# A two-block transformer kernel: the order of ScalarE's and VectorE's pieces in the second block's projections, one pair of gate-row loads on another queue, and two weight blobs exchanged

## What is computed

```python
proj = u @ w_in[l]
qa, ka, va, qb, kb, vb, g = jnp.split(proj, SPLITS, axis=-1)
qa = rope(qa.reshape(B, Lp, SWA_Q_HEADS, HEAD_DIM), pos)      # 16 heads of 64
ka = rope(ka.reshape(B, Lp, SWA_KV_HEADS, HEAD_DIM), pos)     # 4 heads
qb = rope(qb.reshape(B, Lp, DIFF_HEADS, 2, HEAD_DIM), pos)    # 8 heads, two parts each
kb = rope(kb.reshape(B, Lp, DIFF_HEADS, 2, HEAD_DIM), pos)
...
o_swa = windowed_gqa_sink_attention(qa, ka, va, attn_sink[l], pos, is_real)
lam = (jnp.exp(jnp.sum(lambda_q1 * lambda_k1)) - jnp.exp(jnp.sum(lambda_q2 * lambda_k2)) + lambda_init)
o_diff = differential_attention(qb, kb, vb, lam, lambda_init, diff_subln_gain[l], is_key)
gates = jax.nn.sigmoid(g + b_gate[l])
g_swa, g_diff = gates[..., :D_MODEL], gates[..., D_MODEL:]
merged = g_swa * (o_swa @ w_branch_swa[l]) + g_diff * (o_diff @ w_branch_diff[l])
h = h + rms_norm(merged @ w_out[l], post_mix_gain[l])
```

## Time and profile before

| | |
|---|---|
| median of three runs | 875.66 us (875.16 to 877.67) |
| the profiled execution, its own time | 876.87 us |
| its span, first to last instruction | 875.1 us |
| TensorE busy in it | 862.2 us, 99% |
| VectorE, ScalarE, GpSimd busy | 629.0, 468.0, 73.7 us |
| mean granted TensorE clock | 0.999 of full speed |
| HBM traffic | 184 GB/s over the span |

### The profile page before, as it was taken

One profiled execution on the slowest core, in us unless ns is written; L12 is line 12 of the kernel. 1 busy time (PEld: TensorE's weight loads), 2 busy tenths in 40 slices (PEclk: granted clock), 3 DMA queues, 4 the chain that ended last, 5 costly groups with the idle time before them and its releaser, 6 DMA issues.

```text
span 875.1 us, 13099 instructions
## 1 busy us (share of the span) xinstructions
PE 862.2 (99%) x4820; PEld 737.9 (84%) x4820; DVE 629.0 (72%) x985; ACT 468.0 (53%) x756; POOL 73.7 (8%) x96
## 2 busy tenths in 40 slices
PE   8999999999999999999999999999999999999997
PEld 6887788888888888889889888788888888888886
DVE  5867677766876666668778887888766876666665
ACT  6546534434644444444566887676653654444443
POOL 1000000000200000002322010133300100000000
PEclk9999999999999999999999999999999999999999
DMA  9955344554565555352798443755474365455531
GB/s 331 400 212 192 116 169 149 192 188 149 186 241 191 192 192 192 144 192 86 259 274 288 136 157 117 246 192 172 169 269 173 122 225 190 177 198 188 189 143 48
DMA packets 31774, 167.21 MB, mean 191 GB/s; under 512 B 4128, under 2 KB 5920, under 8 KB 14320
## 3 DMA queue, kind: packets, MB, share of 16 engines
q1 hardware_dynamic: 28992, 159.17, 51.8%
q10 hardware_dynamic: 2736, 7.42, 2.4%
HBM read 157.02 MB, written 3.83 MB: 184 GB/s over the span
## 4 chain that ended last, share of the span: by engine, by line
PE 86%; DVE 6%; ACT 3%; DMA 1%; issue 1%; POOL 1%; SPq 0%; ACTq 0%; DVEq 0%
PE ps L522 16%; PE ps L524 16%; PE ps L523 16%; PE ps L688 8%; PE ps L673 8%; PE ps L692 4%; PE ps L669 4%; PE ps L701 2%; DVE wlo L1859 2%; ACT whi L862 1%; PE ps L557 1%; PE ps L1755 1%; DMA kswap<-kraw 1%; PE ps L703 1%; PE ps L1713 1%
## 5 line engine op out<-in xcount | busy, mean ns | idle before, releaser
L1859 DVE TENSOR_TENSOR wlo<-raw,whi 128x2048 fp32r<-128x2048 f32 x134 | 307.4, 2295 | 146.3 <-ACT whi L862 145.9
L862 ACT ACTIVATE whi<-raw 128x2048 fp32r<-128x2048 f32 x134 | 256.2, 1913 | 180.0 <-PE ps L524 109.0
L522 PE MATMUL ps<-whi,xT 128*128 128x512 f32 x192 | 76.8, 400 | 0.0
L524 PE MATMUL ps<-whi,xT 128*128 128x512 f32 x192 | 75.0, 391 | 0.0
L523 PE MATMUL ps<-wlo,xT 128*128 128x512 f32 x192 | 74.8, 390 | 0.0
L1326 POOL TENSOR_TENSOR stat<-stat,cst 128x1 f32<-128x1 f32 x10 | 11.9, 1200 | 490.0 <-DVE stat L1879 261.0
L522 PE MATMUL ps<-whi,fT_h 128*128 128x512 f32 x128 | 50.2, 392 | 0.0
L523 PE MATMUL ps<-wlo,fT_h 128*128 128x512 f32 x128 | 49.8, 389 | 0.0
L524 PE MATMUL ps<-whi,fT_l 128*128 128x512 f32 x128 | 49.8, 389 | 0.0
L522 PE MATMUL ps<-x_all,whi 128*128 128x272 f32 x160 | 46.5, 291 | 1.6 <-DVE wlo L1859 1.5
L523 PE MATMUL ps<-x_all,whi 128*128 128x272 f32 x160 | 46.1, 288 | 0.0
(11 more groups left out here) (349 smaller groups left out, 1886.9 us busy)
## 6 DMA issues: line engine op xcount, KB each, us to landing
raw<-weights SPq DMA_DIRECT2D x134, 1024.0 KB, 4.8
kB<-key_parts SPq DMA_DIRECT2D x20, 272.0 KB, 3.5
kswap<-kraw SPq DMA_DIRECT2D x26, 136.0 KB, 2.5
key_parts<-knat SPq DMA_DIRECT2D x4, 544.0 KB, 7.3
cst<-consts SPq DMA_DIRECT2D x1, 1371.0 KB, 13.3
raw<-weights SPq DMA_DIRECT2D x4, 256.0 KB, 5.1
raw<-weights SPq DMA_DIRECT2D x2, 512.0 KB, 6.7
gate_a<-gain_rows ACTq DMA_DIRECT2D x2, 512.0 KB, 7.9
```

The costliest lines, as they stand in the source:

```text
L522: pe.matmul(o, lh, rh, start=first, stop=False)
L524: return pe.matmul(o, ll, rh, start=False, stop=last)
L862: act.activation(whi[s][:], raw[s][:], ACT.Copy).then_inc(split_hi, 1)
L1859: dve.tensor_tensor(wlo[s][:], raw[s][:], whi[s][:], ALU.subtract).then_inc(split_lo, 1)
```

## The change

1. ScalarE: `keys_high` at q = 4, 6, 8, 10, 12 goes from ahead of the unit's pieces to behind the high part of the same q.
2. ScalarE: `queries_high` goes from ahead of the unit's pieces to behind them, at the same odd q.
3. The gate rows 2 are issued by SyncE, behind the key loads of blob step 22, in place of ScalarE at q = 38. The wait for 16 units' scores is there already, in `load_keys(1)`.
4. Blob 11 becomes a query blob and blob 12 a values blob; `VALUES_AT` moves the turn of these values from q = 24 to 26, and `TAKERS` follows.
5. VectorE: `step_lambda` goes from q = 14 to q = 13, where it stands ahead of the low part of blob 8.

What is computed stays the same, and so do the number and the shapes of all operations.

```diff
--- before.py
+++ after.py
@@ -108,13 +108,13 @@
     return 2 * KC * r + 2 * XT_ORDER[r].index((t, k // 2 * 2)) + k % 2 + 1
 
 
-QUERIES = (6, 7, 9, 10, 12, 13, 15, 17)
+QUERIES = (6, 7, 9, 10, 11, 13, 15, 17)
 QUERY_PLACE = (0, 1, 4, 2, 3, 5, 6, 7)
-VALUES = (5, 8, 11, 14, 16)
+VALUES = (5, 8, 12, 14, 16)
 SWAPPED = (0, 1, 2, 3, 4) + QUERIES
 
 
-VALUES_AT = {12: 0, 18: 1, 24: 2, 30: 3, 34: 4}
+VALUES_AT = {12: 0, 18: 1, 26: 2, 30: 3, 34: 4}
 
 
 def pair_bank(m2):
@@ -484,7 +484,7 @@
 
 
         TAKERS = "aadd" + "aa" + "dd" + "dddd" + "dd" + "dd" + (
-            "aaaaa" + "a" + "dd" + "a" + "dd" + "a" + "dd" + "a" + "d" + "a" + "d" + "dd" + "dd" + "dd" + "dd")
+            "aaaaa" + "a" + "dd" + "a" + "ddd" + "a" + "d" + "a" + "d" + "a" + "d" + "dd" + "dd" + "dd" + "dd")
 
         def wait_pair_free(pe, group):
 
@@ -838,6 +838,9 @@
                     load_keys(0)
                 if 22 <= m < 29:
                     load_keys(m - 21)
+                if m == 22:
+                    for t in range(NT):
+                        sp.dma_start(gate_s[:, t, :], grow[5].partition_broadcast(P)).then_inc(bias_in[2], 16)
                 if m - 7 in QUERIES:
                     store_queries(m - 7)
                 if m - 4 in SWAPPED:
@@ -1150,10 +1153,6 @@
                     values_in(VALUES_AT[q - 1])
                 if q in VALUES_AT:
                     values_out(VALUES_AT[q])
-                if q in (4, 6, 8, 10, 12):
-                    keys_high(q // 2 - 2)
-                if q % 2 == 1 and (q - 5) // 2 in QUERIES:
-                    queries_high((q - 5) // 2)
                 if q == 14:
                     act.wait_ge(lam_s, 1)
                     act.activation(lam[:, 2:4], lam[:, 0:2], ACT.Exp).then_inc(lam_e, 1)
@@ -1204,9 +1203,8 @@
                     act.activation(dT_h[:, cc, t * P:(t + 1) * P], ps[:, 5, 3 * P:4 * P],
                                    ACT.Copy, scale=subgain[:]).then_inc(d_hi, 1)
 
-                if q == 38:
-                    act.wait_ge(u_sc, S_UNITS)
-                    bias_rows(2, gate_s)
+                if q % 2 == 1 and (q - 5) // 2 in QUERIES:
+                    queries_high((q - 5) // 2)
                 if q == 54:
                     act.wait_ge(u_sc, UNITS)
                     bias_rows(3, gate_d)
@@ -1220,6 +1218,8 @@
                     act.dma_start(gain_rows[:], grow[1:3].partition_broadcast(P)).then_inc(rows_in, 16)
                 if q % 2 == 0 and m:
                     hi(N1 + m + 2)
+                if q in (4, 6, 8, 10, 12):
+                    keys_high(q // 2 - 2)
                 if q == 2:
                     for t in range(NT):
                         act.wait_ge(h_ok, 9 + 2 * t)
@@ -2351,7 +2351,7 @@
 
             for q in range(2 * OUT2):
                 m2 = q // 2
-                if q == 14:
+                if q == 13:
                     step_lambda()
                 if q == 4:
                     take_rows(rrow2, 2, 5)
```

## The result

The changed kernel takes 880.26 us (median of 9 runs), the kernel before, run beside it, 875.66: a ratio of 1.0045, with a 95% interval from 1.0036 to 1.0054. By that ratio it is slower by about 4 us (the two medians lie 4.6 apart), and it lies above the predicted range of 872.6 to 878.9. The profiled execution takes 881.04 us, with a span of 879.3 in place of 875.1.

A forecast was written before the change was run, and what follows sets the result against it. TensorE was taken to bound the kernel, busy 862.2 of 875.1 us, with 4.6 us of waits to win. Terms +2.5 - 0.6 - 0.8 = +1.1 us gave a median of 876.8 us, range 872.6 to 878.9.

The forecast's parts named there:

- Weights parts ahead of key parts, q = 4 to 12: ScalarE's reordering: 0 at q = 4, TensorE's 1.5 us wait staying; about 1.5 us won at 443.6 (q = 12).
- my two signs of being wrong: Wrong if the wait at 488 isn't there, or if the swap of blob 6 lands before 453.
- What becomes of these 1.5 us: At blob 8's values, 457 to 458 us: TensorE, early, waits for a transfer, so only 0.3 of 1.5 us are left.
- the lambda step: VectorE, q = 14 to 13: swap of blob 6 issued 0.9 us later, priced at 0 as transfers land in issue order.
- Queries behind the exponentials, blobs 11 and 12 exchanged: q = 23 to 26: a longer chain makes TensorE reach unit 2 at 489.1, not 486.58; a loss of 2.5 us.
- What comes back: TensorE's waits at q = 30 and q = 40 go, winning 0.6 and 0.8 us.
- rival 3: `step_lambda` passes its wait on: swap of blob 6 lands 0.9 later, q = 40 keeps 0.8; +2.8, 878.5 us; chance 0.15.
- Rival 1: q = 20 to 24: query behind the exponentials is out of the way in time; -1.7, 874.0 us; chance 0.26.
- rival 2: Early gains kept: GpSimd isn't held at 417, everything runs 1.1 us ahead; -3.4, 872.3 us; chance 0.14.

The follow-up runs named there:

- keys_alone: Kernel before with only the key parts put behind the weights parts (q = 4 to 12): 878.81 us, ratio 1.0025.
- keys_last_only: Kernel before with only the last key part (q = 12) put behind the high part of blob 8: 875.14 us, ratio 0.9982.
- exchange_alone: Kernel before with only query blob 12 and values blob 11 exchanged: 878.06 us, ratio 1.0012.
- lambda_alone: Kernel before with only the lambda step at q = 13 in place of 14: 876.44 us, ratio 1.0000.
- low5_swap3_first: Kernel before plus changes 1 to 3, blob 3's swap ahead of weights, blob 5's low part ahead of the turn of keys 2: 877.51 us, ratio 1.0007.
- after_swap_first: Changed kernel with stores of keys 1 and 2 and swaps of blobs 3 and 4 ahead of weights of blobs 7 and 8: 876.46 us, ratio 1.0003.
- after_swap3_first: Changed kernel with only the store of keys 1 and the swap of blob 3 ahead of the weights of blob 7: 876.01 us, ratio 0.9994.
- after_queries_back: Changed kernel with the query parts back ahead of the exponentials, blobs 11 and 12 still exchanged: 879.80 us, ratio 1.0035.

## Why the prediction was wrong

**The step that failed** is "Weights parts ahead of key parts, q = 4 to 12". Up to blob 5 it was right almost to the figure: GpSimd's part took 2.65 (2.64 forecast), the turn of keys 2 started at 423.51 + 1.5 = 425.0 (425.1), the low part of blob 5 at 427.1 (427.2). Behind that I followed nothing until q = 12 and entered a gain of 1.5, of which 0.3 was to last. But GpSimd's part of keys 1 ended earlier (422.64 + 1.5 = 424.1, in place of 425.7), while the weights of blob 7 were issued 1.3 later, so its store and the swap of blob 3 went out right behind 1 MB of weights. The term was -1.5 for one wait; measured, that wait of 1.7 gave way to two with 3.7 in all, and the step alone costs 2.2 us (keys_alone). Taken back from the whole change it makes 3.3. Neither of my two signs of being wrong came up, as both look past this step: the wait at q = 26 is there, and the swap of blob 6 lands at 452.7 + 1.5 = 454.2.

**"What becomes of these 1.5 us"** failed too. With the wait gone, the gain stays (keys_last_only: -1.6), since the swap of blob 6 lands 3.2 us after its issue and doesn't hold TensorE at 458. I had taken landings of one execution for fixed times: behind the same transfers at the same distances the swap took 3.0 in exchange_alone. Nor did all transfers of that execution land in the order of issue, on which the 0 for the lambda step rested: the first half of this swap, issued at 446.61, landed after 3.1 us, at 449.7, ahead of the weights (451.1) and the keys (452.5).

**Queries behind the exponentials, blobs 11 and 12 exchanged:** the place was right and the size nearly so (a wait on the copy of values at q = 26, 1.8 for 2.3 forecast; 0.2 for 0.8 at 481). The cause was one of the two edits that the term priced together: the exchange puts the values at the end of a chain through the low part of blob 14 and unit 2's scaling, and makes the wait by itself (1.9 in exchange_alone), wherever query 10's copies stand. Without the exchange the queries' move, with the gate rows on SyncE, gains 1.1.

**What comes back** was right: no wait at q = 30 and 40. **The lambda step** at 0 agrees with lambda_alone; its interval doesn't rule out the 0.9 of rival 3, but the wait that this rival needs isn't there. Rival 1 fell with the wait at q = 26, and rival 2 with GpSimd's part, which was held (2.65 us); early gains came only with another order on SyncE.

**TensorE's clock** was no term at all. In the profile of after it accounts for most of what the waits don't: 5.7 us behind the start-up, against 3.0 more of waits. Sum of the forecast +1.1; measured about +4: 3.3 from the key parts and 0.6 from the rest, both with the clock in them. So the forecast was near for the rest, and what it lacked is the key parts. The parts don't simply add: timed alone they give +2.2, +1.1, -1.1 and 0, in sum 2.2.

## What to carry to other kernels

When an engine's work ends sooner, the transfers that hang on it are issued sooner too: look up what the queue holds ahead of them at that moment, since here a small transfer that others waited for came late behind a megabyte that nobody needed yet. Read how long a transfer takes from more than one profile before a step rests on it. Follow every link of a chain that is moved, not only the one at which a wait stood. When two edits of a change pull in different directions, time them apart: here the parts that gain, with the swaps put ahead of the weights, are worth 3.9 us without the others.

## What the runs showed of the hardware

The fall of the granted clock differs between executions of one kernel. In the 126 runs of the kernel before that were made beside the experiments, the mean granted clock was 0.998 or higher in 86 (median 876.0 us) and lower in 40 (877.7). Across kernels the share tends to go with the longest wait of the profile: lower in 0 of 12 for keys_last_only, whose longest wait is 1.5, in 7 of 9 for the changed kernel (2.4), in 10 of 11 for low5_swap3_first (4.6). But the waits don't settle it: after_swap_first and after_swap3_first have the same two of 1.9 in their profiles and are lower in 9 of 12 and 3 of 11. The three waits of 1.9 to 2.3 in the profile of after_queries_back had no fall behind them (granted clock 1.00 from 425 to 500). So a wait of about 2 us cost its length and, in some executions, up to about 1.7 us more (the windows of the changed kernel, and 877.7 against 876.0).
